# Re-ordering the opening of the attention projection (na_in) in a one-core fp32 transformer kernel

## The reference

```
x   = x   + gx2 * mlp(modulate(rms(x,   norm_mlp_g[0]), sx2, cx2), w1[0], w2[0])   # layer 0
ctx = ctx + gc2 * mlp(modulate(rms(ctx, norm_mlp_g[0]), sc2, cc2), w1[0], w2[0])
...
hx = modulate(rms(x, norm_mix_g[1]), sx1, cx1)                                     # layer 1
hc = modulate(rms(ctx, norm_mix_g[1]), sc1, cc1)
q   = rms(heads(hx @ wq), q_g);  k   = rms(heads(hx @ wk), k_g);  v   = heads(hx @ wv)
k_c = rms(heads(hc @ wk), k_g);  v_c = heads(hc @ wv)
x = x + gx1 * (neighbourhood_attention(q, k, v, k_c, v_c, rpb) @ na_w_out)
```

## Time and profile before

| what | value |
|---|---|
| three runs, median | 1298.64 us (1298.61 to 1300.02) |
| the profiled execution, its time | 1300.44 us |
| its span, first to last instruction | 1298.6 us |
| PE busy | 1280.0 us (99%) |
| PE weight loads busy | 1107.6 us (85%) |
| DVE, ACT, POOL busy | 948.5, 594.6, 449.4 us |
| PE idle for DVE, ACT or POOL at the opening of na_in | 0.70, 0.49, 2.60 us |

### The profile page before, as it was taken

How to read it: one execution, slowest core, us unless ns; L and a number is a source line. 1 busy time by engine, 2 the same in 40 slices (tenths; PEclk the granted TensorE clock), 3 DMA queues, 4 the chain that set the end, 5 groups by cost and what they waited for, 6 DMA issues and landing times.

```text
span 1298.6 us, 20165 instructions
## 1 busy us (share of the span) xinstructions
PE 1280.0 (99%) x7856; PEld 1107.6 (85%) x7856; DVE 948.5 (73%) x1366; ACT 594.6 (46%) x960; POOL 449.4 (35%) x434
## 2 busy tenths in 40 slices
PE   9999999999999999999999999999999999999999
PEld 8888989999888888888788787889677777999887
DVE  6688698999897898896567576566577765855553
ACT  6237556666653332444212244124455554666432
POOL 1572132333330012375200266012456552488200
PEclk9999999999999999999999999999999999999999
DMA  8774465565562653354355465563232321555552
GB/s 305 260 266 154 151 209 199 183 187 183 204 221 95 210 195 115 113 178 162 127 191 192 156 227 194 192 222 137 81 108 72 114 96 55 194 186 186 184 190 81
DMA packets 66270, 220.00 MB, mean 169 GB/s; under 512 B 9120, under 2 KB 12448, under 8 KB 66176
## 3 DMA queue, kind: packets, MB, share of 16 engines
q1 hardware_dynamic: 65888, 218.46, 50.1%
q10 hardware_dynamic: 288, 0.25, 0.1%
HBM read 217.21 MB, written 1.05 MB: 168 GB/s over the span
## 4 chain that ended last, share of the span: by engine, by line
PE 76%; DVE 14%; issue 5%; DMA 2%; ACT 2%; POOL 1%; SPq 0%; DVEq 0%; ACTq 0%; POOLq 0%
PE ps L630 17%; PE ps L642 17%; PE ps L644 16%; PE ps L620 8%; DVE wlo L1887 4%; PE ps L622 4%; DVE tmp L2177 2%; DMA raw<-in_w_in 2%; PE ps L1216 1%; DVE Y L1914 1%; PE ps L1243 1%; PE ps L1230 1%; DVE modsum L1969 1%; PE ps L1209 1%; PE ps L716 1%
## 5 line engine op out<-in xcount | busy, mean ns | idle before, releaser
L630 PE MATMUL ps<-A,whi 128*128 128x256 f32 (+2 forms) x1508 | 490.0, 325 | 0.0
L644 PE MATMUL ps<-A,wlo 128*128 128x256 f32 (+2 forms) x1488 | 472.5, 318 | 1.8 <-DVE wlo L1887 1.8
L642 PE MATMUL ps<-A,whi 128*128 128x256 f32 (+2 forms) x1488 | 472.1, 317 | 0.2 <-DVE A L1900 0.2
L1382 ACT ACTIVATE whi<-raw 128x1024 fp32r<-128x1024 f32 (+1 forms) x302 | 317.1, 1051 | 301.8 <-DMA raw<-in_w_0b 77.8
L1887 DVE TENSOR_TENSOR wlo<-raw,whi 128x1024 fp32r<-128x1024 f32 (+1 forms) x302 | 402.4, 1337 | 47.9 <-ACT whi L1382 47.5
L630 PEld LDWEIGHTS ps<-A,whi 128*128 128x128 f32 x1508 | 286.3, 190 | 42.2 <-issue 19.9
L644 PEld LDWEIGHTS ps<-A,wlo 128*128 128x128 f32 x1488 | 282.4, 190 | 21.8 <-DVE wlo L1887 2.6
L642 PEld LDWEIGHTS ps<-A,whi 128*128 128x128 f32 x1488 | 282.9, 190 | 20.0 <-issue 1.4
L1969 DVE SCALAR_TENSOR_TENSOR modsum<-raw,cond,modsum 128x1024 f32<-128x1024 f32 x98 | 150.7, 1567 | 0.0
L2615 POOL TENSOR_TENSOR H<-tmp,H 128x256 fp32r<-128x256 f32 (+1 forms) x86 | 127.0, 1477 | 66.2 <-ACT H L1714 52.7
L620 PE MATMUL ps<-H,whi 128*128 128x512 f32 x400 | 140.4, 396 | 0.2 <-POOL H L2615 0.2
(11 more groups left out here) (355 smaller groups left out, 1672.6 us busy)
## 6 DMA issues: line engine op xcount, KB each, us to landing
raw<-in_ada SPq DMA_DIRECT2D x96, 512.0 KB, 3.9
raw<-in_w SPq DMA_DIRECT2D x64, 512.0 KB, 3.5
raw<-in_w_up SPq DMA_DIRECT2D x44, 512.0 KB, 3.5
raw<-in_w_in SPq DMA_DIRECT2D x34, 512.0 KB, 5.8
raw<-in_w_0a SPq DMA_DIRECT2D x32, 512.0 KB, 4.0
raw<-in_w_0b SPq DMA_DIRECT2D x32, 512.0 KB, 3.5
raw<-in_na_in SPq DMA_DIRECT2D x24, 512.0 KB, 5.0
raw<-in_w_down SPq DMA_DIRECT2D x22, 512.0 KB, 4.0
```

The lines of the kernel that those rows point to most:

```text
L630: e.matmul(o, w_hi, ah, start=k == 0, stop=False)
L642: e.matmul(o, w_hi, al, start=False, stop=False)
L644: m = e.matmul(o, w_lo, ah, start=False, stop=last)
L1382: e.activation(whi[s % NHI][:, :cols], raw[i % NRAW][:, :cols], ACT.Copy).then_inc(S("whi").sem, 1)
```

## The change

- `MOD_AFTER`: two modulation tiles that were loaded and accumulated behind the last two units of w2_0a now follow units 13 and 15 of w1_0a; those between move up by two places.
- `MOD_SUMMED`: the last modulation sum moves from behind chunk 3 of na_in to behind chunk 6 of w2_0b. Its transposes stay at chunk 4 of na_in.
- The second spread of row factors (`column_rows("na", 1)`) stands behind three instead of six channel tiles of chunk v0's high products.
- DVE makes the low tiles by channel (both halves of tile 2, then of tile 3, ...), and PE does the low products of k0, q0 and v0 side by side for each channel tile, instead of chunk after chunk.
- The head sum of k0 moves from the middle of v0's low products to the middle of chunk k1, that of q0 from there to the end of k1, the v0 transposes from the end of k1 to the end of q1.
- On DVE, the outputs of k0 and q0 both come at chunk 3, and the copy of the transposed v0 comes behind unit 4's split.

```
-MOD_AFTER = {... "w1_0a": (1, 2, 4, 5, 7, 8, 10, 11),
-             "w2_0a": range(16), ...
+MOD_AFTER = {... "w1_0a": (1, 2, 4, 5, 7, 8, 10, 11, 13, 15),
+             "w2_0a": range(14), ...
-MOD_SUMMED = {..., ("w1_0b", 14): 5, ("na_in", 3): 6}
+MOD_SUMMED = {..., ("w1_0b", 14): 5, ("w2_0b", 6): 6}
...
+        def na_low(k):
+            if k in LOW_P:
+                w.wait_ge(S("na_lp"), 3 + k)
+            else:
+                w.wait_ge(S("na_lo"), 2 * (k - 1))
...
-        high_half("na_in", (2,), 0, ready("na_hi"), range(6))
+        high_half("na_in", (2,), 0, ready("na_hi"), range(3))
         column_rows("na", 1)
-        high_half("na_in", (2,), 0, ready("na_hi"), range(6, 8))
+        high_half("na_in", (2,), 0, ready("na_hi"), range(3, 8))
...
-        low_part("na_in", 0, 512, both_low("na"))
-        low_part("na_in", 1, 256, x_low("na"))
-        low_part("na_in", 2, 512, both_low("na"), midway=lambda: during_na(1))
+        for k in range(8):
+            na_low(k)
+            for n, T in ((0, 512), (1, 256), (2, 512)):
+                m = e.matmul(bank_of("na_in", n)[:, :T], weights_of("na_in", n, k)[0], Alo[:, k, :T], start=False, stop=k == 7)
+                if k == 7:
+                    m.then_inc(S("mm").sem, 1)
 
         def midway_na(n):
             if n == 3:
-                during_na(2)
+                during_na(1)
             after_na(n - 1)
 
+        def end_na(n):
+            if n == 4:
+                during_na(3)
+            during_na(n - 1 if n == 3 else n)
...
         for c in range(2, 8):
-            shifted_lo("na", c, 0, 1, 0)
-        for c in range(2, 8):
-            shifted_lo("na", c, 1, 1, 0)
+            for q in range(2):
+                shifted_lo("na", c, q, 1, 0)
...
-            if norm2(n - 2):
-                j, dst, T = norm2(n - 2)
-                head_out(j, T, dst, param("q_g" if j % 2 else "k_g"))
+            for m in () if n == 2 else (0, 1) if n == 3 else (n - 2,):
+                if norm2(m):
+                    j, dst, T = norm2(m)
+                    head_out(j, T, dst, param("q_g" if j % 2 else "k_g"))
...
-                values_before(i)
+                if i not in (3, 4):
+                    values_before(i)
                 if i:
                     los(UNIT["na_in", i])
+                if i == 4:
+                    values_before(3)
```

More of the change, by code:

```diff
@@ L57 @@
 FIRST = {16: 0, 17: 0, 32: 0, 33: 1, 48: 2, 49: 3, 64: 4, 65: 4, 80: 5, 81: 5}
-MOD_AFTER = {"w_down": (1, 3, 15, 17, 19), "ab_in": (3, 4, 5, 6, 6, 7, 8, 9, 10, 11, 12, 13, 14), "ab_out": range(6), "w1_0a": (1, 2, 4, 5, 7, 8, 10, 11),
-             "w2_0a": range(16), "w1_0b": (2, 3, 4, 4, 5, 6, 7, 7, 8, 9, 10, 10, 11, 12, 13, 13),
+MOD_AFTER = {"w_down": (1, 3, 15, 17, 19), "ab_in": (3, 4, 5, 6, 6, 7, 8, 9, 10, 11, 12, 13, 14), "ab_out": range(6), "w1_0a": (1, 2, 4, 5, 7, 8, 10, 11, 13, 15),
+             "w2_0a": range(14), "w1_0b": (2, 3, 4, 4, 5, 6, 7, 7, 8, 9, 10, 10, 11, 12, 13, 13),
              "w2_0b": (0, 1, 2, 3, 3, 4, 5, 6, 6, 7, 8, 9, 9, 10, 11, 12)}
 SUMS = [(0, None), (1, None), (2, 0), (2, 1), (3, None), (4, None), (5, None)]
-MOD_SUMMED = {("ab_out", -1): 1, ("w1_0a", 13): 3, ("w1_0b", 1): 4, ("w1_0b", 14): 5, ("na_in", 3): 6}
+MOD_SUMMED = {("ab_out", -1): 1, ("w1_0a", 13): 3, ("w1_0b", 1): 4, ("w1_0b", 14): 5, ("w2_0b", 6): 6}
 ADA_WRITTEN = {("w_in", 34): 0, ("ab_out", 0): 1, ("w1_0a", 15): 3, ("w1_0b", 2): 4, ("w1_0b", 15): 5, ("na_in", 4): 6}
@@ L702, in low_half, with low_part @@
                 m.then_inc(S("mm").sem, 1)
-        def low_part(name, n, T, lo_ready, midway=None):
+        def low_part(name, n, T, lo_ready):
             for k in range(8):
-                if midway and k == 4:
-                    midway()
                 lo_ready(k)
@@ L1225, in turned2 @@
                     bank = ps[7]
-                    w.wait_ge(S("ada_copy"), 6)
+                    w.wait_ge(S("ada_copy"), 7)
                     w.wait_ge(S("p2_pt1"), 2 * p + b)
@@ L1270, in after_na @@
                 scores2(*scores)
-        low_part("na_in", 0, 512, both_low("na"))
-        low_part("na_in", 1, 256, x_low("na"))
-        low_part("na_in", 2, 512, both_low("na"), midway=lambda: during_na(1))
+        for k in range(8):
[4 more added lines that the diff above has]
+                    m.then_inc(S("mm").sem, 1)
         def midway_na(n):
             if n == 3:
-                during_na(2)
+                during_na(1)
             after_na(n - 1)
+        def end_na(n):
+            if n == 4:
+                during_na(3)
+            during_na(n - 1 if n == 3 else n)
         linear("na_in", lambda n: 256 if NA_CHUNKS[n][0] == "q" else 512, lambda k: (Ahi[:, k], Alo[:, k]), all_ready("na_hi", 16),
-               both_low("na"), during=during_na, midway=midway_na, begin=3)
+               na_low, during=end_na, midway=midway_na, begin=3)
         def out_part(n, pairs):
```

## The result

| | before | after |
|---|---|---|
| median, us | 1299.27 (16 runs, 1297.62 to 1301.43) | 1302.92 (16 runs, 1301.13 to 1306.83) |
| ratio to before | | 1.0027, interval 1.0018 to 1.0035 |
| the profiled execution, its time and span | 1300.44, 1298.6 | 1301.79, 1299.7 |
| mean granted clock over the runs | 0.9988 (92 runs beside the experiments) | 0.9968 (16 runs) |
| runs with mean clock 1.000 | 31 of 92 | 0 of 16 |

The change makes the kernel 3.5 us slower (2.3 to 4.5). The forecast of 1299.9 was wrong, and 1302.92 lies above the range. Of the rivals (b) is the nearest (1302.6): its two stretches at half level came at the last transposes, but half of them fell in the idle, and a third one behind another wait made up the price.

What follows compares the result with a forecast made beforehand. PE's own work was taken as the bound, with 6.6 us of waits and half clock in na_in's opening to win. Gains handed back at one wait: +0.3 + 1.2 - 0.2 = +1.3 on 1298.64, 1299.9 us; range 1297.1 to 1302.3.

Steps and rivals of the forecast that it cites:

- (b): Rival, slower: idle at the last transposes long enough for two half-level stretches; price 4.0, 1302.6 us; chance 0.19.
- The moved sum: In w2_0b behind chunk 6, between full-speed products: costs about 1.0 us, against 1.87 at half clock in na_in.
- The low products and the wait behind them: Opening of na_in: low products end at 912.8 without waits, then 1.1 us idle before k1 for ScalarE's square of k0.
- The modulation transposes: Last ones in na_in: PE waits 4 to 5.5 us for DVE's copy out of ps6, until about 930.9.
- The collisions: DVE and GpSimd blocking each other on SBUF reads in na_in: the chain to the copy ends at 931.15, without them 929.85.
- (a): Rival, gain kept: no wait at the last transposes, k2 5 us ahead, 1293.7 us; chance 0.09 with other kept gains.
- (c): Rival: PE still waits for v0 behind q0's logarithm and exponential; +1 to +1.5 us; chance 0.72 together with the forecast.
- its second term, the clock: Half-level stretch behind the wait at the last transposes: 1.2 us taken, bounds 0 and, with two stretches, 3.4.
- sign of being wrong: Near or behind the last transposes: half speed lasting beyond 5 us would show the forecast wrong, on the slower side.
- Chunk k2: Its start in na_in: 932.25 against 931.98 before, +0.3 us, between -0.8 and +0.6 by the collisions.
- The third term: Wait of 0.67 us at the second scores (942.59) may shrink: -0.2 us taken, between 0 and -0.67.
- 1.7 us of half clock saved: Behind the 2.60 us idle at the v0 transposes: 3.4 us at half speed, costing up to 1.7, would go.

Runs made afterwards that it cites:

- x11: Kernel before, with one edit: in na_in DVE's mean of the newer head stands ahead of the older head's output; 1292.00 us, ratio to before 0.9940.
- x2: Changed kernel with 20 products that compute nothing of use filling PE's wait at the last modulation transposes; 1300.52 us, ratio to before 1.0015.
- x3: Kernel before with 10 products that compute nothing of use filling PE's wait ahead of the v0 transposes; 1298.56 us, ratio to before 0.9997.
- x7: x1 plus k1's mean before unit 4's split, k0's low products earlier, k1's head sum behind three k2 products; 1298.00 us, ratio to before 0.9991.
- x1: Changed kernel with DVE's copy of v0 put ahead of the outputs of k0 and q0; 1299.15 us, ratio to before 1.0002.

## Why the prediction was wrong

**The steps up to the last transposes held.** The moved sum takes 0.99 us in w2_0b (882.98 to the next product at 883.97; 1.0 was said). There is no idle at the context half. The low products and the wait behind them take 5.68 us (907.33 to 913.01; 5.76 said), with 0.82 of idle for ScalarE's square of k0 (1.1 said). The v0 transposes do not wait. The modulation transposes wait 4.92 us for the copy (4 to 5.5 said), and start at 930.12 + 1.98 = 932.10, against a forecast of 930.9 + 1.0 = 931.9. (The 0.74 us of like steps that the prediction sets beside GpSimd's 1.80 is not among; the trace of before has it at 960.18.) The collisions on which this rested are in the rows: DVE's split of 920.63 took 2.14 against 1.22, and GpSimd's third step of k0 1.47, where the step in x11 took 0.62 with no split beside it. Rivals (a) and (c) fell with this.

**The sum failed at its second term, the clock.** The text took 1.2 us, "bounds 0 and, with two stretches, 3.4". The profiled execution paid nearly the upper bound: the four transposes and the first six products of k2 ran at half level. That cost 0.38 and 1.29 us more than at full (930.12 to 930.86 for 0.36; the first 12 products, 930.86 to 935.09, for 2.94, which is what lies between 931.98 and the first scores at 934.92 in the trace of before), and the second stretch at 943.9, behind the wait of 0.69 at the scores, brought 1.58 (from the third score product to a later one, 940.95 to 958.33, against 940.80 to 956.60). That is 3.25. Over the runs it is less sure: 6 of the 16 have a mean clock as low as the profiled one's 0.996, and x2 puts the price at 1.6 to 2.6. The reason given for less, that part of a stretch passes in the idle, is true (3.3 of the first 6.8 us), but the half level lasted that much longer: 6.8 us and then 3.4, beyond the 5 us that the prediction names as its sign of being wrong. The second stretch is a term that the sum did not have: it stands behind the wait at the scores, not behind the long one.

**The other terms.** Chunk k2 starts 0.86 later than before (930.86 + 1.98 against 931.98); 0.3 was said, bounds -0.8 to 0.6, and 0.38 of the difference is the half clock on the transposes. The third term, -0.2 for the wait at the second scores, did not come: 0.69 against 0.67. In sum the trace gives +0.86 + 1.29 + 1.58 and an unchanged wait, +3.7, of which 0.6 comes back by the second v transposes (962.25 + 1.98 against 961.08): +3.15, within the interval of the runs.

**What one trace could not tell.** The kernel before was credited with 1.7 us of half clock saved. That was in its profiled execution; over its runs the loss is smaller (x3: 0.4 to 0.95). The change gives up a price that is paid two times in three at most; of its own 16 runs none has a mean clock of 1.000. Nor is this all the clock. Against a before that pays no half clock, the other terms of the sum would make 0.3 + 1.7 = 2.0, as the 1.7 is not there to be saved. The runs agree: the 8 of x2 with a mean clock of 1.000 take 1300.35 on average, the 11 of before beside them 1298.00, so the wait alone costs 2.3.

A rule bears on the copy's place behind the outputs. The Trainium skill (TensorE: Matmul & The Clock Gate, "Architectural detail: the array is 16× 32×32, not 1× 128×128") says in its paragraph on queue depths that ScalarE and VectorE take their instructions in strict first-in, first-out order. The trace agrees: DVE idled 1.87 and 1.92 us ahead of the outputs, and for the last 1.1 us of the first and all of the second the copy's data were there (v0's transposes ended at 923.56).

## What to carry to other kernels

On an engine that works in order, look for short rows that others wait for and that stand behind a long row or one which waits for a slow engine: here a mean of 0.42 us and a copy of 0.69. Swapping mean and output in the kernel before brought 7.8 us, while the change, which re-ordered TensorE's work, left the later means behind the outputs and put the copy there too, lost 3.5. What is won ahead of such a wait can be handed back at it (the change itself, x7), and idle on TensorE is to be priced with the half clock that may follow, over several executions and not one.

## What was not expected of the hardware

A wait of 0.69 us was followed by 3.4 us at the 1.2 GHz level in the profiled execution of after (943.9), and one of 0.61 in x1 (934.4), where waits of 0.67 in the kernel before and 0.7 in x2, at the same place as that of after, left the clock at 1.00. What sets the one from the other, and why a third of the runs of before have a mean clock of 1.000, stays open. So does the spread of after: 8 of its 16 runs lie between 1301.1 and 1302.3, the others between 1303.6 and 1306.8, with mean clocks of 0.996 to 0.999 in the first group and 0.995 to 0.999 in the second.
